# Forget-gate chain of the first head pair moved one token tile earlier, and the decay rows' transfer moved behind three stores

## The chip, the cores and the metric

The program runs on one core of a Trainium2 chip. The metric is the device time of one execution in microseconds; the median of three runs is given. TensorE (PE in the views) multiplies, VectorE (DVE), ScalarE (ACT) and GpSimd (POOL) work elementwise, and SyncE (SP) issues nearly all DMA transfers. Each engine runs its own instructions in program order and waits on semaphores that the other engines raise.

## The reference, cut to what matters

One layer of a hybrid encoder is computed for 1024 prompt tokens and for 8 running streams of 16 tokens with 512 cached tokens each. The part around the change is attention with a forget gate, for 8 heads of width 64:

```python
proj = rms_norm(x, ln1) @ w_in
q, k, v, f, xr, yg = jnp.split(proj, SPLITS, axis=-1)
q = rms_norm(q.reshape(B, T, N_HEADS, HEAD_DIM), q_gain)
k = rms_norm(k.reshape(B, T, N_HEADS, HEAD_DIM), k_gain)
logf = jax.nn.log_sigmoid((f + b_f).astype(jnp.float32))
c = jnp.cumsum(logf, axis=1)
# logit[t,s] = q_t.k_s/sqrt(d) + c_t - c_s, for s <= t
```

After it come a gated recurrence on the other half of the width, an output projection and an MLP of width 4096. The forget values `logf`, their running sums and the normed keys are outputs or operands of the attention.

## The kernel before, in words

The 1152 tokens are nine tiles of 128 (tile 8 holds the streams' tokens). The heads are worked through in four pairs, `p` = 0 to 3. For a pair, TensorE projects tile after tile to queries, keys and values (`project(t)`, 24 matmuls of 384 columns, in four quarters; `amid(t, quarter)` puts other work between the quarters). ScalarE copies the values and squares queries and keys (`sqj`), VectorE sums the squares (`mean(t)`, L1577 and L1578), GpSimd takes the power of -1/2 (L794), VectorE scales queries and keys (`norm(t)`, L1589 and L1591), and TensorE transposes them (`turn_qk(t)`, L2236 and L2237). `turn_qk(t - 1)` stands behind `project(t)`; for `t = 4` it stands behind `project(5)`, and right behind it stands `bound(0, 0)` (L2256), the first product of the turned queries and keys. That product reads the rows of `KA` that hold the running forget sums, and so waits for `c_rows_in`.

Only in pair 0, the forget gate is worked out beside this. `turn(t)` transposes the normed input tiles, ScalarE and VectorE split them in two parts (`turn_hi`, `turn_lo`), `forgets(g)` (16 matmuls, L2094 and L2095) multiplies a third of the tokens with the gate's weights and waits for the low parts of its three tiles, `forget_rows(g)` copies the result, `turn_inputs` (L2101) transposes it. VectorE then computes log-sigmoid in about twenty small operations (`forget_sizes`, `forget_values`, L1460 to L1484), with one exponential on ScalarE in between. `turn_forgets` (L2109, L2113) transposes the values, `prompt_sums` (L1490, L1492) takes the running sums, `prompt_rows` (L1497, L1498) splits them in two parts, `own_sums` (L1504) and `sample_sums` (L1511 to L1521) do the same for the streams. SyncE writes the split rows to a scratch array in device memory (L634, L635), waits for it, and loads two rows per head into `KA` (`decay_rows(0)`, L593).

The order on each engine is the order in which the code is written; there is no planner. SyncE's order in pair 0 is: the nine stores of the forget values (L512), the store of the normed keys of tiles 0 and 1 (`keys_out`, L588, each waits for `norm` of its tile), the two writes and two loads of the decay rows, `keys_out` of tiles 2, 3 and 4, and then the copies of queries and keys that the scores need (`duplicates`, L603 and L604).

Of the kernel before, what the change touches and what calls it, by code (L numbers as in the profile page):

```python
# [7 lines left out]
F32 = mybir.dt.float32  # L8
# [12 lines left out]
H = 8  # L21
# [37 lines left out]
def streaming_step(nc, x_prompt, x_sample, cache_k, cache_v, cache_logf, state_h, state_conv, ln1, w_in, b_f,  # L59
# [36 lines left out]
    c_row = sb(over, "c_row", [40, SEQ], F32R)  # L96
# [134 lines left out]
    c_dram = nc.dram_tensor("c_scratch", [H, 2, SEQ], F32).ap()  # L231
# [272 lines left out]
    with nc.allow_non_contiguous_dma(reason="narrow columns of small arrays"), nc.Block() as block:  # L504

        @block.sync
        def _(sp):
# [83 lines left out]
            def decay_rows(p):  # L591
                for hp in range(2):
                    sp.dma_start(KA[DECAY_ROWS[hp], hp, :].bitcast(F32), c_dram[2 * p + hp]).then_inc(c_rows_in, 16)  # L593
# [32 lines left out]
            def pair_transfers(p):  # L626
                last = p == PAIRS - 1
                keys_out(p, 0)
                if p >= 1:
                    denominators(p - 1)  # L630
                keys_out(p, 1)
                if p == 0:
                    sp.wait_ge(c_split, 1)
                    sp.dma_start(c_dram[:, 0, :], c_row[0:H, :].bitcast(F32)).then_inc(c_saved, 16)  # L634
                    sp.dma_start(c_dram[:, 1, :], c_row[32:32 + H, :].bitcast(F32)).then_inc(c_saved, 16)  # L635
                    sp.wait_ge(c_saved, 32)
                    sp.wait_ge(operands_set, 2)
                    decay_rows(0)
                if p >= 1:
                    sp.wait_ge(s_scores, 2 * p)  # L640
                    past_values(p - 1, 1)
                keys_out(p, 2)
                if p >= 1:
                    quotients(p - 1)
                    for b in range(2):
                        past_keys(p, b)
                keys_out(p, 3)
                keys_out(p, 4)
                if p == 0:
                    sp.wait_ge(stored, 16 * n_stored)  # L650
                    sp.wait_ge(consts_ready, 3)
                duplicates(p, 0)
                for t in range(5, NT):
                    keys_out(p, t)
                    if t == 6 and not last:
                        for j in range(4):
                            sp.wait_ge(w_lo, 4 * p + j + 1)
                            pair_weights(p + 1, j)
                    if t == 6 and last:
                        for u in range(2):  # L660
                            sp.wait_ge(w_lo, 4 * p + u + 1)
                            lru_weights(0, u)
                if p == 0:
                    sp.wait_ge(c_past_ready, 1)
                    for b in range(2):
                        past_keys(0, b)
                duplicates(p, 1)
                sp.wait_ge(v_done, NT * p + NT)
                sp.dma_start(v_prompt[0, 0].rearrange("(t p) h d -> p t h d", p=P)[:, :, 2 * p:2 * p + 2, :].rearrange(
                    "p t h d -> p t (h d)"), v1[:]).then_inc(v_out, 16)  # L670
                sp.dma_start(v_sample[0].rearrange("b t h d -> (b t) h d")[:, 2 * p:2 * p + 2, :],
                             v_own[:].rearrange("p (h d) -> p h d", h=2)).then_inc(v_out, 16)
                for b in range(2, 6):
                    sp.wait_ge(kc_turned, DEC_B * p + b - 1)
                    past_keys(p, b)
                sp.wait_ge(den_done, 6 * p + 6)
                past_values(p, 0)
                if not last:
                    decay_rows(p + 1)
                for b in range(6, DEC_B):  # L680
                    sp.wait_ge(kc_turned, DEC_B * p + b - 1)
                    past_keys(p, b)
                if last:
                    for b in range(4):
                        sp.dma_start(v_last[:, b, :].rearrange("p (t n) -> p t n", t=KP),
                                     cache_v[0, 4 + b, :, 2 * p:2 * p + 2, :].rearrange("(t p) h d -> p t (h d)", p=P)
                                     ).then_inc(vk_in, 16)
# [278 lines left out]
        def _(act):  # L966
# [24 lines left out]
            def first_stage(i):  # L991

                if i == 0:
                    square(0)
                    square(1)
                    turn_hi(0)
                    pair_hi(0, 0)
                    square(2)
                    turn_hi(1)
                    for j in range(1, 4):  # L1000
                        pair_hi(0, j)
                    square(3)
                    turn_hi(2)
                    act.wait_ge(wf_in, 16)
                    nc.scalar.copy(wf[:, :, 0, :], wf_raw[:]).then_inc(wf_split, 1)
                    square(4)
                    turn_hi(3)
                if i == 1:
                    square(5)
                    turn_hi(4)  # L1010
                    square(6)
                    turn_hi(5)
                    square(7)
                    forget_rows(0)
                    turn_hi(6)
                    square(8)
                    forget_rows(1)
                    turn_hi(7)
                    turn_hi(8)
                if i == 2:  # L1020
                    forget_rows(2)
                    act.wait_ge(l_abs, 1)
                    nc.scalar.activation(l_e[:], l_e[:], ACT.Exp, scale=-1.0).then_inc(l_exp, 1)
# [353 lines left out]
        def _(dve):  # L1377
# [35 lines left out]
            def first_stage(i):  # L1413


                if i == 0:
                    for t in range(5):
                        x_mean_of(t)
                        if t >= 2:
                            turn_lo(t - 2)  # L1420
                        if t == 0:
                            dve.wait_ge(ln1_in, 16)
                        x_norm(t)
                        if t == 2:
                            for j in range(4):
                                pair_lo(0, j)
                            dve.wait_ge(wf_split, 1)
                            nc.vector.tensor_tensor(wf[:, :, 1, :], wf_raw[:], wf[:, :, 0, :].bitcast(F32),
                                                    ALU.subtract).then_inc(wf_ready, 1)
                if i == 1:  # L1430
                    x_mean_of(5)
                    dve.wait_ge(small_in, 16 * SMALL)
                    nc.vector.tensor_scalar(qgain[:], qgain[:], DH ** -0.5, None, ALU.mult)
                    dve.wait_ge(rows_turned, 1)
                    nc.vector.tensor_copy(param[:, :, 0:ROWS], psum[:, 5, 0:LC * ROWS].rearrange(
                        "p (c r) -> p c r", c=LC)).then_inc(params_copied, 1)
                    turn_lo(3)
                    x_norm(5)
                if i == 2:
                    for t in (6, 7, 8):  # L1440
                        x_mean_of(t)
                        turn_lo(t - 2)
                        x_norm(t)
                    past_sums()
                    turn_lo(7)
                    turn_lo(8)

            def past_sums():

# [122 lines left out]
            def pair_dve(p):  # L1572
# [85 lines left out]
                for t in range(NT):  # L1658
# [10 lines left out]
                            low_keys(0, hp)  # L1669
                    bounds_ahead(t)  # L1670
                    mean(t)
                    if p == 0 and t == 3:
                        prompt_sums()
                    bounds_behind(t)
                    if p == 0 and t == 0:
                        first_stage(1)
# [1 line left out]
                    if t == 6:  # L1678
                        bound(1, 0)
                    if p == 0 and t == 1:  # L1680
                        forget_sizes()
                        forget_values()
                    if p == 0 and t == 3:
                        prompt_rows()
                        own_sums()
                        sample_sums()
                    if p >= 1 and t == 2:
                        invert(p - 1)
# [351 lines left out]
        def _(pe):  # L2040
# [22 lines left out]
            def first_stage(i):  # L2063
# [4 lines left out]
                if i == 1:  # L2068
# [14 lines left out]
                        last = nc.tensor.transpose(psum[0:64, f_bank(0), kt * P:(kt + 1) * P], cl[:, kt, :], ident[:])  # L2083
                    last.then_inc(c_turned, 1)
                    turn(8)

            def forgets(g):

# [111 lines left out]
            def pair_pe(p):  # L2200
# [130 lines left out]
                        bound(0, 5)  # L2331

                def amid(t, quarter):
                    if p == 0 and (t, quarter) == (2, 0):
                        turn_inputs()
                    if p == 0 and (t, quarter) == (3, 2):
                        turn_forgets()
                    bounds_amid(t, quarter)
                    if (t, quarter) == (8, 2):
                        turn_qk(7)  # L2340

                for t in range(NT):
                    if p == 0:
                        first_stage(t)
                    project(t, amid)
                    if p == 0 and t == 1:
                        forgets(2)
                    if p >= 1:
                        samples_meanwhile(p - 1, t)
                    if 1 <= t < 8:  # L2350
# [330 lines left out]
```

## Time and profile before

| | us |
|---|---|
| median of three runs | 1426.71 (1425.75 to 1428.8) |
| the profiled execution's own time | 1428.8 |
| its span in the trace | 1427.1 |
| TensorE busy | 1369.3 (96%) |
| VectorE busy | 1003.8 (70%) |
| ScalarE busy | 522.7 (37%) |
| GpSimd busy | 389.7 (27%) |

The span is the stretch from the first to the last recorded instruction. A busy share is an average over stages: the first 111 us, in which the changed code lies, have other limits than the MLP that fills the second half. The chain of waits follows the end of the program back through whatever released each step; 85% of the span stands on it for TensorE.

### The profile page before, as it was taken

The page shows a single profiled execution, that of the slowest core. Times are in us where ns is not written, and L with a number is a line of the kernel's source. Part 1 is how long each engine was busy: PE and PEld are TensorE (multiplying, and loading weights), DVE is VectorE, ACT ScalarE, POOL GpSimd, SP SyncE. Part 2 cuts the span into 40 slices and gives each one's busy share as a digit, 9 for nine tenths or more (in the row PEclk, how much of TensorE's full clock was granted, in tenths as well). Part 3 has the DMA queues.
Part 4 walks back from the last instruction along what each step waited for, and adds up shares of the span by engine and source line. Part 5 has one row for each costly group of instructions (what it writes and reads, how often), then busy time and mean ns, then how long its engine had stood idle before and what let it go on. Part 6 is the DMA issues. An engine that isn't in the chain of part 4 may idle for free.

```text
span 1427.1 us, 21431 instructions
## 1 busy us (share of the span) xinstructions
PE 1369.3 (96%) x7479; PEld 1168.0 (82%) x7487; DVE 1003.8 (70%) x1523; ACT 522.7 (37%) x964; POOL 389.7 (27%) x396
## 2 busy tenths in 40 slices
PE   5989999999899999999999999999999999999998
PEld 4765847839658887788999999999999999999997
DVE  6763453543624566765888898888888898888885
ACT  5224242342335555332532343334433343334330
POOL 5310101101100002101532454345433553255320
PEclk9999999999999999999999999999999999999999
DMA  6042333424343032012201110111101110121004
GB/s 200 12 115 74 89 80 111 106 65 113 77 128 84 3 105 87 33 47 89 60 6 53 59 59 27 32 59 59 47 12 59 59 59 0 59 59 59 0 30 133
DMA packets 129544, 92.90 MB, mean 65 GB/s; under 512 B 14678, under 2 KB 119126, under 8 KB 129492
## 3 DMA queue, kind: packets, MB, share of 16 engines
q1 hardware_dynamic: 129492, 92.20, 22.6%
q8 instruction: 33, 0.54, 0.2%
q14 instruction: 19, 0.16, 0.0%
HBM read 78.28 MB, written 9.71 MB: 62 GB/s over the span
## 4 chain that ended last, share of the span: by engine, by line
PE 85%; DVE 5%; DMA 4%; ACT 3%; issue 1%; POOL 1%; SPq 1%; DVEq 0%; POOLq 0%
PE psum L2043 16%; PE psum L2045 15%; PE psum L2044 15%; PE psum L2523 8%; PE psum L2525 8%; PE psum L2524 8%; DMA k_c<-in_cache_k_dram 3%; PE psum L2305 2%; PE psum L2256 2%; PE psum L2287 1%; PE psum L2290 1%; PE psum L2315 1%; PE psum L2414 1%; PE psum L2126 1%; DVE tops L1611 1%
## 5 line engine op out<-in xcount | busy, mean ns | idle before, releaser
L1909 DVE TENSOR_TENSOR mix<-mix,psum 128x512 f32<-128x512 f32 x660 | 417.8, 681 | 92.0 <-PE psum L2525 87.6
L2043 PE MATMUL psum<-h_hi,wu_hi 128*128 128x384 f32 x768 | 259.4, 338 | 0.9 <-DVE wu_lo L1874 0.9
L2045 PE MATMUL psum<-h_hi,wu_lo 128*128 128x384 f32 x768 | 258.1, 336 | 0.0
L2044 PE MATMUL psum<-h_lo,wu_hi 128*128 128x384 f32 x768 | 258.1, 336 | 0.0
L2523 PE MATMUL psum<-wd_hi,u_hi 128*128 128x512 f32 x516 | 201.3, 390 | 0.2 <-DVE mix L1909 0.2
L2525 PE MATMUL psum<-wd_hi,u_lo 128*128 128x512 f32 x516 | 200.7, 389 | 0.0
L2524 PE MATMUL psum<-wd_lo,u_hi 128*128 128x512 f32 x516 | 200.7, 389 | 0.0
L2043 PEld LDWEIGHTS psum<-h_hi,wu_hi 128*128 128x128 f32 x768 | 144.3, 188 | 10.0 <-issue 1.3
L2044 PEld LDWEIGHTS psum<-h_lo,wu_hi 128*128 128x128 f32 x768 | 144.3, 188 | 8.7
L2045 PEld LDWEIGHTS psum<-h_hi,wu_lo 128*128 128x128 f32 x768 | 144.4, 188 | 0.0
L1265 ACT CAST wd_hi<-raw 128x512 fp32r<-128x512 f32 x109 | 67.1, 621 | 179.7 <-PE psum L2525 81.2
L1255 ACT ACTIVATE up<-psum 128x384 f32<-128x384 f32 x96 | 46.8, 487 | 203.0 <-PE psum L2045 167.8
L914 POOL TENSOR_TENSOR up<-up 128x384 f32<-128x384 f32 x15 | 21.1, 1404 | 345.1 <-DVE u_lo L1885 345.1
L2525 PEld LDWEIGHTS psum<-wd_hi,u_lo 128*128 128x128 f32 x516 | 96.9, 188 | 20.6
L2523 PEld LDWEIGHTS psum<-wd_hi,u_hi 128*128 128x128 f32 x516 | 96.9, 188 | 11.9 <-DVE mix L1909 0.6
L2524 PEld LDWEIGHTS psum<-wd_lo,u_hi 128*128 128x128 f32 x516 | 96.9, 188 | 11.2
L2043 PE MATMUL psum<-wp_hi,h_hi 128*128 128x384 f32 x288 | 103.2, 359 | 0.0
L1880 DVE TENSOR_TENSOR wd_lo<-raw,wd_hi 128x512 fp32r<-128x512 f32 x109 | 93.8, 873 | 8.3 <-ACT wd_hi L1265 4.6
L2044 PE MATMUL psum<-wp_lo,h_hi 128*128 128x384 f32 x288 | 98.0, 340 | 0.0
L2045 PE MATMUL psum<-wp_hi,h_lo 128*128 128x384 f32 x288 | 97.9, 340 | 0.0
L794 POOL TENSOR_TENSOR rs<-m,neg_half 128x4 f32<-128x4 f32 x36 | 36.3, 1008 | 190.0 <-DVE m L1578 190.0
L1885 DVE TENSOR_TENSOR u_lo<-up,u_hi 128x768 fp32r<-128x768 f32 (+1 forms) x62 | 75.2, 1213 | 6.2 <-ACT u_hi L1303 5.3
(321 smaller groups left out, 2460.8 us busy)
## 6 DMA issues: line engine op xcount, KB each, us to landing
raw<-in_w_up_dram SPq DMA_DIRECT2D x32, 512.0 KB, 5.9
raw<-in_w_down_dram SPq DMA_DIRECT2D x32, 512.0 KB, 4.4
k_c<-in_cache_k_dram SPq DMA_DIRECT2D x32, 256.0 KB, 2.9
raw<-in_w_in_dram SPq DMA_DIRECT2D x32, 192.0 KB, 4.0
out_dram<-mix SPq DMA_DIRECT2D x9, 512.0 KB
v_c<-in_cache_v_dram SPq DMA_DIRECT2D x16, 256.0 KB, 4.2
raw<-in_w_in_dram SPq DMA_DIRECT2D x8, 512.0 KB, 5.4
raw<-in_w_out_dram SPq DMA_DIRECT2D x8, 512.0 KB, 4.1
```

The source lines that it names most:

```text
L794: nc.gpsimd.tensor_tensor(rs4[:, t % 2, :], m4[:, t % 2, :], neg_half[:], ALU.pow).then_inc(rs4_ready, 1)
L1255: nc.scalar.activation(up[:, into, :], psum[:, bank(m), 0:GN], ACT.Relu).then_inc(up_read, 1)
L1265: nc.scalar.copy(wd_hi[:, slot, :], src).then_inc(wd_rounded, 1)
L1880: nc.vector.tensor_tensor(wd_lo[:, slot, :], src, wd_hi[:, slot, :].bitcast(F32), ALU.subtract).then_inc(wd_ready, 1)
L1885: nc.vector.tensor_tensor(lo, src, hi.bitcast(F32), ALU.subtract).then_inc(u_ready, 1)
L1909: nc.vector.tensor_tensor(half_of(t, half), half_of(t, half), psum[:, product_bank(n), :].rearrange("p (k n) -> p k n", n=P), op).then_inc ...
L2043: nc.tensor.matmul(out, hi(k), r_hi(k), start=first and k == 0, stop=False)
L2044: nc.tensor.matmul(out, hi(k), r_lo(k), start=False, stop=False)
L2045: last = nc.tensor.matmul(out, lo(k), r_hi(k), start=False, stop=end and k == n - 1)
L2523: nc.tensor.matmul(psum[:, bank, :], u_hi, wd_hi[:, w, :], start=first, stop=False)
L2524: nc.tensor.matmul(psum[:, bank, :], u_hi, wd_lo[:, w, :], start=False, stop=False)
L2525: return nc.tensor.matmul(psum[:, bank, :], u_lo, wd_hi[:, w, :], start=False, stop=end)
```

## The change

Nothing is computed in another way; the same instructions are issued in another order on TensorE, ScalarE, VectorE and SyncE, all within pair 0.

```diff
# SyncE, pair_transfers
                 keys_out(p, 1)
-                if p == 0:
-                    sp.wait_ge(c_split, 1)
-                    sp.dma_start(c_dram[:, 0, :], c_row[0:H, :].bitcast(F32)).then_inc(c_saved, 16)
-                    sp.dma_start(c_dram[:, 1, :], c_row[32:32 + H, :].bitcast(F32)).then_inc(c_saved, 16)
-                    sp.wait_ge(c_saved, 32)
-                    sp.wait_ge(operands_set, 2)
-                    decay_rows(0)
...
                 keys_out(p, 3)
                 keys_out(p, 4)
                 if p == 0:
+                    sp.wait_ge(c_split, 1)
+                    sp.dma_start(c_dram[:, 0, :], c_row[0:H, :].bitcast(F32)).then_inc(c_saved, 16)
+                    sp.dma_start(c_dram[:, 1, :], c_row[32:32 + H, :].bitcast(F32)).then_inc(c_saved, 16)
+                    sp.wait_ge(c_saved, 32)
+                    sp.wait_ge(operands_set, 2)
+                    decay_rows(0)
                     sp.wait_ge(stored, 16 * n_stored)
                     sp.wait_ge(consts_ready, 3)
                 duplicates(p, 0)
# ScalarE, first_stage
                     turn_hi(8)
-                if i == 2:
                     forget_rows(2)
                     act.wait_ge(l_abs, 1)
                     nc.scalar.activation(l_e[:], l_e[:], ACT.Exp, scale=-1.0).then_inc(l_exp, 1)
# VectorE, first_stage(2), called ahead of mean(1)
                     turn_lo(8)
+                    forget_sizes()
+                    forget_values()
# VectorE, loop over tiles
                     mean(t)
-                    if p == 0 and t == 3:
-                        prompt_sums()
...
                     norm(t)
...
                     if p == 0 and t == 1:
-                        forget_sizes()
-                        forget_values()
-                    if p == 0 and t == 3:
+                        prompt_sums()
                         prompt_rows()
                         own_sums()
+                    if p == 0 and t == 3:
                         sample_sums()
# TensorE, first_stage(1), called ahead of project(1)
                     turn(8)
+                    forgets(2)
# TensorE, amid
-                    if p == 0 and (t, quarter) == (2, 0):
+                    if p == 0 and (t, quarter) == (1, 0):
                         turn_inputs()
-                    if p == 0 and (t, quarter) == (3, 2):
+                    if p == 0 and (t, quarter) == (2, 2):
                         turn_forgets()
# TensorE, loop over tiles
                     project(t, amid)
-                    if p == 0 and t == 1:
-                        forgets(2)
```

On SyncE, in the transfers of pair 0, the rows before are these (`c_row` holds the split running sums, `qk` the normed queries and keys of a tile):

```order
L512 DMA out_dram<-l_f 128x8 x9
L588 DMA out_dram<-qk 128x128 x2
L634 DMA c_scratch<-c_row 8x1024
L635 DMA c_scratch<-c_row 8x1024
L593 DMA KA<-c_scratch 2x1024 x2
L588 DMA out_dram<-qk 128x128 x3
L603 DMA cross_qk<-QA 64x512
```

And these are the rows of the changed kernel:

```order
L512 DMA out_dram<-l_f 128x8 x9
L588 DMA out_dram<-qk 128x128 x5
L644 DMA c_scratch<-c_row 8x1024
L645 DMA c_scratch<-c_row 8x1024
L593 DMA KA<-c_scratch 2x1024 x2
L603 DMA cross_qk<-QA 64x512
```

The decay rows' four transfers stand behind the key stores of tiles 2, 3 and 4, no longer ahead of them.

On VectorE, behind the small operations of the forget values, the rows before are these (each pair L1577, L1578 is a `mean`, each pair L1589, L1591 a `norm`; the first ones here are those of tile 2):

```order
L1484 TENSOR_SCALAR param<-param 128x4x2
L1577 TENSOR_REDUCE s<-sqj 128x4
L1578 TENSOR_SCALAR m<-s 128x4
L1589 TENSOR_TENSOR qk<-psum,rs 128x256
L1591 TENSOR_TENSOR qk<-qk,kgain 128x128
L1577 TENSOR_REDUCE s<-sqj 128x4
L1578 TENSOR_SCALAR m<-s 128x4
L1490 SCALAR_TENSOR_TENSOR cp<-ones_w,psum 8x512
L1492 SCALAR_TENSOR_TENSOR cp<-ones_w,cp,psum 8x512
L1589 TENSOR_TENSOR qk<-psum,rs 128x256
L1591 TENSOR_TENSOR qk<-qk,kgain 128x128
L1497 TENSOR_SCALAR c_row<-cp 8x1024
```

And in the changed kernel, where the first `mean` and `norm` are those of tile 1:

```order
L1484 TENSOR_SCALAR param<-param 128x4x2
L1577 TENSOR_REDUCE s<-sqj 128x4
L1578 TENSOR_SCALAR m<-s 128x4
L1589 TENSOR_TENSOR qk<-psum,rs 128x256
L1591 TENSOR_TENSOR qk<-qk,kgain 128x128
L1490 SCALAR_TENSOR_TENSOR cp<-ones_w,psum 8x512
L1492 SCALAR_TENSOR_TENSOR cp<-ones_w,cp,psum 8x512
L1497 TENSOR_SCALAR c_row<-cp 8x1024
L1498 SCALAR_TENSOR_TENSOR c_row<-cp,c_row 8x1024
L1504 TENSOR_REDUCE c_new<-psum 64x16
L1577 TENSOR_REDUCE s<-sqj 128x4
L1578 TENSOR_SCALAR m<-s 128x4
```

The small operations now stand ahead of tile 1's `mean`, which was ahead of them, and the running sums stand in one block behind tile 1's `norm`, ahead of tile 2's `mean`.

## Rows read from the trace of the kernel before

**Rows 1.** Busy times by stretch: length, PE, PEld, DVE, ACT, POOL, PEclk, DMA.
```profile
69.60:73.70 4.10, 0.00 (x0) 0.00 (x0) 2.77 (x7) 0.65 (x2) 1.01 (x1) 1.00 0.13 36
73.70:78.10 4.40, 4.36 (x18) 4.33 (x19) 4.09 (x8) 0.00 (x0) 0.61 (x1) 0.61 0.58 134
```

**Rows 2.** Chain of waits, 40 to 112 us: start, length, engine, tile, line.
```profile
70.73 0.48 DVE c_past L1521
...
71.89 1.02 POOL rs L794
```

**Rows 3.** TensorE's timeline: start, length, engine, line; in brackets idle before, releaser.
```profile
29.17 1.97 PE L2059 MATMUL psum<-ident,x_more 128*128 128x128 f32 x8 [2.82 <-DVE x_more L1389]
...
41.30 1.09 PE L2059 MATMUL psum<-ident,x_in 128*128 128x128 f32 x8 [1.35 <-DVE x_in L1389]
...
46.41 0.33 PE L2094 MATMUL psum<-h_hi,wf 128*16 128x384 f32 x1
...
50.56 0.72 PE L2101 MATMUL psum<-ident,f_rows 16*128 16x16 f32 x9
...
57.81 1.03 PE L2109 MATMUL psum<-ident,l_f 128*8 128x128 f32 x8
...
60.30 0.27 PE L2236 MATMUL psum<-ident,qk 128*128 128x128 f32 x1
...
69.25 0.34 PE L2045 MATMUL psum<-wp_hi,h_lo 128*128 128x384 f32 x1
73.74 0.33 PE L2236 MATMUL psum<-ident,qk 128*128 128x128 f32 x1 [4.16 <-DVE qk L1591]
...
73.93 0.30 PE L2256 MATMUL psum<-KA,QA 128*128 128x128 f32 x1
```

**Rows 4.** VectorE's timeline.
```profile
42.30 2.45 DVE L1396 TENSOR_TENSOR h_lo<-psum,h_hi 128x512 fp32r<-128x512 f32 x4
...
51.33 0.23 DVE L1460 TENSOR_TENSOR l_in<-psum,bf_b 128x72 f32<-128x72 f32 x1 [1.47 <-PE psum L2101]
...
57.20 0.42 DVE L1577 TENSOR_REDUCE s<-sqj 128x4 f32<-128x256 f32 x1
...
61.62 1.20 DVE L1490 TENSOR_TENSOR_SCAN cp<-ones_w,psum 8x512 f32<-8x512 f32 x1
...
64.16 0.43 DVE L1589 TENSOR_TENSOR qk<-psum,rs 128x256 f32<-128x256 f32 x1
...
64.83 0.67 DVE L1497 TENSOR_SCALAR c_row<-cp 8x1024 fp32r<-8x1024 f32 x1
...
67.11 0.24 DVE L1511 TENSOR_TENSOR_SCAN cc_new<-ones_w,cc,c_new 64x16 f32<-64x16 f32 x1
...
71.14 0.41 DVE L1577 TENSOR_REDUCE s<-sqj 128x4 f32<-128x256 f32 x1
...
73.39 0.29 DVE L1591 TENSOR_TENSOR qk<-qk,kgain 128x128 f32<-128x128 f32 x1
```

**Rows 5.** ScalarE's timeline, the squares of tile 3.
```profile
60.66 0.39 ACT L1090 ACTIVATE sqj<-psum 128x256 f32<-128x256 f32 x1
```

**Rows 6.** GpSimd's timeline, the end of the second stream mask.
```profile
52.06 0.38 POOL L855 CAST smask<-build 128x128 bf16<-128x128 f32 x1
```

**Rows 7.** SyncE's timeline: start and length of the issues.
```profile
66.78 0.30 SPq L634 DMA_DIRECT2D c_scratch<-c_row  x1
67.12 0.29 SPq L635 DMA_DIRECT2D c_scratch<-c_row  x1
69.22 0.52 SPq L593 DMA_DIRECT2D KA<-c_scratch  x2
...
73.71 0.33 SPq L588 DMA_DIRECT2D out_dram<-qk  x1
```

**Rows 8.** The key stores' view: issue to landing, 55 to 112 us.
```profile
out_dram<-qk SPq DMA_DIRECT2D x9, 64.0 KB, 1.6
```

**Rows 9.** Chain of waits, the longest load of cached keys.
```profile
134.58 4.67 DMA k_c<-in_cache_k_dram
```

## The prediction

> **What bounds the kernel now.** I read the page first: TensorE is busy for 96% of the span, so only its idle stretches and its slow stretches can change the time, and an edit on another engine counts only if it makes or removes such a stretch. Then I read TensorE's timeline from the start to 111 us, where all the changed code runs. Between the end of the input tiles' transposes and the first attention product it has one large hole: `project(5)` ends at 69.25 + 0.34 = 69.59, and `turn_qk(4)` starts at 73.74, after 4.16 us of idle [rows 3]. The table by stretch shows the same, and that the clock granted in the next stretch, 4.40 us long, is 0.61 of full, a mixture of the 1.2 and the 2.4 GHz level [rows 1]. That stretch loses 4.40 x (1 - 0.61) = 1.7 us. Hole and slow stretch together are 5.9 us; this is all that the change could win there.
>
> The chain of waits says what ends the hole: VectorE's `sample_sums` end at 70.73 + 0.48 = 71.2, then `mean(4)`, GpSimd's power (1.02 us), `norm(4)` [rows 2], which ends at 73.39 + 0.29 = 73.68 [rows 4]. So VectorE's queue is the limit there, not a transfer. `bound(0, 0)` follows at 73.93 [rows 3] without a wait of its own: the decay rows were issued to `KA` by 69.22 + 0.52 = 69.74 [rows 7]. They are not on the path before. I call the end of `norm(4)` N, and compare the start of `bound(0, 0)`, 73.93 before, since everything behind it keeps its order.
>
> **The change part by part.** First, `forgets(2)` ahead of `project(1)`. It waits for the low parts of tile 8. TensorE's transposes end at 41.30 + 1.09 = 42.39 [rows 3], VectorE's four splits at 42.30 + 2.45 = 44.75 [rows 4]. Before, `project(1)` lay in this gap. Now nothing does: TensorE is idle for 2.4 us, with 24 ready projection matmuls queued behind the waiting instruction. This is a new cost.
>
> Second, where this puts the forget chain. From the first matmul of `forgets(2)` to `turn_inputs` the trace has 50.56 - 46.41 = 4.15 us; a `turn_qk` of 0.13 us in it is gone (an estimate, half of the 0.27 us of such a row). So `turn_inputs` starts at 44.8 + 4.0 = 48.8, and VectorE, which starts 51.33 - 50.56 = 0.77 behind it, at 49.6: 1.7 us earlier than the 51.33 of before [rows 3, 4].
>
> Third, VectorE from there to N. The blocks, with their lengths from [rows 4]:
> - forget values: 57.20 - 51.33 = 5.87, to 55.5
> - tile 1, `mean` to the end of `norm`: 73.68 - 71.14 = 2.54 (of which 1.2 us is waiting for GpSimd), to 58.0
> - `prompt_sums`: 64.16 - 61.62 = 2.54, to 60.55
> - `prompt_rows` and `own_sums`: 67.11 - 64.83 = 2.28, to 62.85
> - tile 2: 2.54, to 65.4
> - tile 3: 2.54, to 67.95
> - `sample_sums`: 71.14 - 67.11 = 4.03, to 72.0
> - tile 4: 2.54, so N = 74.55
>
> That is 0.9 us later than 73.68, though the forget chain began 1.7 us earlier. Two things eat the lead: tile 1's `mean` and `norm` now stand behind the forget values instead of ahead of them (2.54 us more), and the two scans no longer lie between `mean(3)` and `norm(3)`, where they covered GpSimd's 1.2 us. Against it, VectorE's wait of 1.3 us for tile 3's squares is gone. None of the blocks has to wait longer for its input: the squares of tile 3 stood ready 60.66 + 0.39 = 61.05, 0.75 us after the `turn_qk(2)` behind that projection began [rows 3, 5], and each projection now ends at least 1 us ahead of its `mean`; `turn_forgets`, at 57.81 before [rows 3], comes 1.7 us earlier and ends, with its last product, near 57.5, ahead of the 58.0 at which the scans want it. GpSimd's second mask ends at 52.44 before [rows 6], and now stands behind tile 1's power, to end near 60.8, ahead of tile 2's `mean` at 62.85.
>
> Fourth, TensorE on the way to N. From 42.39 to `turn_qk(2)` at 60.30 it works without a hole [rows 3], 17.9 us; the same work is there after the change. So it reaches `turn_qk(2)` at 42.39 + 2.4 + 17.9 = 62.7 and there waits for tile 2's `norm` at 65.4: a second new hole of 2.7 us. From there 69.59 - 60.30 = 9.3 us bring it to 74.7, the same moment as N. The hole of 4.16 us ahead of `turn_qk(4)` is really gone, and has been paid for by 5.1 us of holes earlier.
>
> Fifth, the decay rows, the dearest edit. Their four transfers now stand on SyncE behind `keys_out(4)`, which waits for N. `bound(0, 0)` needs them. From N [rows 7]: the key store is issued from 0.03 to 0.36; the two writes to the scratch array take 67.41 - 66.78 = 0.63 and end at 1.03; SyncE then waits for them to land, 69.22 - 67.41 = 1.81, to 2.84; the second load is issued from 3.1. Its landing is not in the trace. The nearest rows bound it: a key store lands 1.6 us after its issue [rows 8], the second scratch write was landed 69.22 - 67.12 = 2.1 us after it began [rows 7], and as an upper end stands the 4.67 us of the longest load of cached keys [rows 9]. The decay load is two rows of one head, far smaller than that, so I take 1.6 to 2.1 and say 1.85. The rows are there at N + 5.0 = 79.55, with 4.67 at 82.3. TensorE has only `turn_qk(4)` to do meanwhile, 0.2 us, so it is idle for about 4.7 us where it was idle for 4.16. I cost the key stores that now go ahead at nothing: nobody but `norm(5)` to `norm(8)` waits for them, over 5 us later.
>
> The Trainium skill, in "DMA: Bandwidth & Descriptors", section "Anatomy of one DMA — SWDGE (gpsimd) path", gives a fixed cost of about 2.0 us for each DMA, nearly all of it the wait for the write's receipt, whatever the size. The 2.1 us of the scratch write [rows 7] agrees; by the page the rows would be there at about N + 5.1, which changes nothing.
>
> **The sum.** `bound(0, 0)` at 79.55 against 73.93: +5.6 us. The same by holes: 2.4 + 2.7 + 4.7 - 4.16 = 5.6. Behind it the slow stretch of 1.7 us stays as it is, since the hole in front of it is no shorter. VectorE is ahead of TensorE there, but what follows the hole is limited by TensorE's projections. So the profiled execution would take 1428.8 + 5.6 = 1434.4. That execution lies 2.1 us above the median of its three runs; for the median I forecast 1426.7 + 5.6 = 1432.3.
>
> **The rivals.**
> - The slow clock comes early. After 2.82 us of idle the eight transposes at 29.17 took 1.97 us, after 1.35 us of idle those at 41.30 took 1.09 [rows 3]. The new hole of 2.4 us follows one of 1.35 with 1.09 of work between, and lies between these two cases. If `forgets(2)` runs at 1.2 GHz, the forget chain and N move by as much: half to all of the 1.7 us of [rows 1], say 1.5. Then 1433.8. The hole at `turn_qk(2)` can slow `project(4)` and `project(5)` too, but TensorE arrives there when the decay rows still need 5 us, so that costs nothing.
>
> The Trainium skill, "TensorE: Matmul & The Clock Gate", section "HAM oscillation — how this bites in real kernels", says that waits between groups of matmuls put the array back to half clock each time, which speaks against two more holes; the 29.17 row agrees, the 41.30 row shows a short wait that did not.
>
> - The clock does not fall at the last hole, and the slow stretch of before goes. For it: the trace shows falls behind 2.82 and 4.16 us of idle and none behind 1.35 [rows 3], too few to call it certain. Against it: 4.7 us is more than either. It gives back 1.7: 1430.6.
> - The shift is swallowed later. Behind pair 0's attention the chain stands on loads of cached keys, up to 4.67 us each [rows 9]. If their end were set by an earlier time than TensorE's, the 5.6 us would vanish in them: 1426.7. Against it: each of these loads waits for the transposes of the load two before it (`kc_turned`), so they move with TensorE. Only the first two are issued freely.
> - The other side: VectorE runs ahead as the order intends, `turn_qk(2)` does not wait, and the decay rows are in place. Then the old 5.9 us go and only the 2.4 us come: 1423.2. It decides at N + 5.0 < 73.9, so N would have to be under 68.9, 5.7 us earlier than worked out; that would need two whole tiles' `mean` and `norm` and more to vanish from VectorE's queue. Nothing in the rows speaks for it except that the forget chain does start earlier.
>
> **How the numbers follow.** The forecast gets 0.55, the early slow clock 0.24, the unchanged fast clock 0.11, the swallowed shift 0.05, the other side 0.04, and 0.01 is for none of them. A change of less than 0.2%, 2.9 us, can't be told from none here. Slower than that are the first two, and most of the third: 0.88. Within it lie the swallowed shift and a bit of the third: 0.08. Faster: 0.04. The range runs from 1429.6 (the third case less 1.0 for the spread of a median) to 1436.0 (the second with a landing nearly 1 us later and the spread). With the upper end of the landing alone the time would be 1435.1, inside it.
>
> **What would show it.** In the changed kernel's profile: an idle of about 2.4 us ahead of the `forgets(2)` matmuls, and of about 2.7 ahead of the third `turn_qk`; `turn_qk(4)` near 74.7 with almost no wait; SyncE's writes to the scratch array at about 75, no longer at 66.8, though `c_row` is ready near 62.5; and a wait of nearly 5 us ahead of the first L2256 row, ended by the DMA into `KA`. It would be wrong if the first L2256 product started before 77, if the decay rows were issued ahead of N, or if the time behind this product grew or shrank by more than 2 us.

## The result and the profile after

The changed kernel takes 1440.31 us (median of four runs, 1440.14 to 1440.63) against 1427.76 for the kernel before on the same chip (four runs, 1425.75 to 1429.01). The ratio is 1.0085 with an interval of 1.0068 to 1.0102: slower, as forecast, but by 12.5 us where 5.6 were forecast, and outside the range given. Two more comparisons of the same two kernels (below) gave 1.0051 and 1.0057, 7.8 and 7.9 us between the medians. The profiled execution takes 1439.09 us (span 1437.4), 10.3 more than the 1428.8 of before; this difference the trace can explain.

The head of the page of the changed kernel shows busy time, share of the span and instructions of each engine:

```profile
span 1437.4 us, 21430 instructions
...
PE 1376.5 (96%) x7479; PEld 1172.7 (82%) x7487; DVE 1003.8 (70%) x1523; ACT 522.7 (36%) x964; POOL 389.7 (27%) x396
```

VectorE and GpSimd are busy for exactly as long as before. TensorE is busy 7.2 us longer than its 1369.3, though its work is the same. So most of what was lost is not waiting: TensorE ran slower.

The table by stretch says where. These are two stretches of the kernel before, cut at the end of `turn(8)` and at the first `bound(0, 0)` product (columns as in [rows 1]):

```profile
42.40:73.90 31.50, 27.23 (x164) 24.32 (x164) 21.04 (x56) 6.57 (x18) 8.97 (x20) 1.00 0.07 13
73.90:113.50 39.60, 35.91 (x196) 25.16 (x195) 26.07 (x46) 11.85 (x29) 4.03 (x4) 0.96 0.39 104
```

And the same two of the changed kernel:

```profile
42.70:82.10 39.40, 31.49 (x166) 27.26 (x165) 24.23 (x61) 6.43 (x18) 9.71 (x21) 0.86 0.07 12
82.10:123.00 40.90, 37.16 (x194) 26.11 (x194) 22.96 (x40) 11.80 (x29) 3.21 (x4) 0.92 0.38 99
```

In the first, the time grows by 7.9 us; 4.3 of these are busy time (27.23 to 31.49) at a granted clock of 0.86 where it was 1.00. In the second it grows by 1.3. The remaining 1.1 us are spread over the rest of the span, 0.3 of them ahead of `turn(8)`.

TensorE's timeline of the changed kernel shows the holes (start, length, tile, count, in brackets the idle time before and what ended it), in answer to [rows 3]:

```profile
41.62 1.09 PE L2056 MATMUL psum<-ident,x_in 128*128 128x128 f32 x8 [1.36 <-DVE x_in L1387]
...
45.21 0.48 PE L2092 MATMUL psum<-h_hi,wf 128*16 128x384 f32 x1 [2.50 <-DVE h_lo L1394]
...
51.72 0.73 PE L2099 MATMUL psum<-ident,f_rows 16*128 16x16 f32 x9
...
68.26 0.47 PE L2234 MATMUL psum<-ident,qk 128*128 128x128 f32 x1 [2.23 <-DVE qk L1591]
...
78.54 0.27 PE L2234 MATMUL psum<-ident,qk 128*128 128x128 f32 x1
82.15 0.48 PE L2254 MATMUL psum<-KA,QA 128*128 128x128 f32 x1 [3.23 <-DMA KA<-c_scratch]
```

The reader is to see three holes, of 2.50, 2.23 and 3.23 us, at the three places named in the prediction, and also that the first matmul behind each of them takes 0.47 or 0.48 us, where the same kinds took 0.33, 0.33 and 0.30 in [rows 3]. The stretches behind them say how long that lasted:

```profile
45.20:50.60 5.40, 5.39 (x17) 2.74 (x18) 0.00 (x0) 0.07 (x1) 0.55 (x2) 0.50 0.00 0
...
68.20:74.40 6.20, 6.14 (x29) 6.11 (x30) 4.71 (x12) 0.06 (x1) 1.01 (x1) 0.74 0.08 21
82.10:88.50 6.40, 6.35 (x22) 5.64 (x23) 2.09 (x6) 0.00 (x0) 0.20 (x1) 0.50 0.40 92
```

0.50 is 1.2 GHz throughout. The losses, length times what is missing from 1.00, are 5.4 x 0.50 = 2.7, 6.2 x 0.26 = 1.6 and 6.4 x 0.50 = 3.2 us; before there was one such stretch, of 1.7. The sum: holes 2.50 + 2.23 + 3.23 - 4.16 = 3.8, slow clock 2.7 + 1.6 + 3.2 - 1.7 = 5.8, together 9.6, against 7.9 + 1.3 = 9.2 by stretch.

VectorE's timeline carries the first of these losses on to N:

```profile
52.48 0.23 DVE L1460 TENSOR_TENSOR l_in<-psum,bf_b 128x72 f32<-128x72 f32 x1 [7.42 <-PE psum L2099]
...
64.07 1.22 DVE L1498 SCALAR_TENSOR_TENSOR c_row<-cp,c_row 8x1024 fp32r<-8x1024 f32 x1
...
74.92 0.42 DVE L1577 TENSOR_REDUCE s<-sqj 128x4 f32<-128x256 f32 x1 [0.23 <-ACT sqj L1088]
...
77.19 0.29 DVE L1591 TENSOR_TENSOR qk<-qk,kgain 128x128 f32<-128x128 f32 x1
```

The forget chain begins at 52.48, not 49.6, and N is 77.19 + 0.29 = 77.48. `c_row` is ready at 64.07 + 1.22 = 65.29. SyncE's timeline shows when it is written out:

```profile
63.01 14.84 SPq L588 DMA_DIRECT2D out_dram<-qk  x5
77.89 0.34 SPq L644 DMA_DIRECT2D c_scratch<-c_row  x1
78.27 0.29 SPq L645 DMA_DIRECT2D c_scratch<-c_row  x1
80.35 0.52 SPq L593 DMA_DIRECT2D KA<-c_scratch  x2
```

The rows lie ready for 12.6 us behind key stores that wait for N, and then the two dependent transfers follow, which the chain of waits times from issue to landing:

```profile
78.27 2.07 DMA c_scratch<-c_row
80.35 0.22 SPq L593
80.62 1.48 DMA KA<-c_scratch
82.15 0.48 PE psum L2254
```

The product starts 82.15 - 77.48 = 4.67 us behind N.

### The profile page after: what moved, and what is told of

It reads as the page before. It is cut to its first block, busy times and chain, and to the rows that moved or that the text cites. A ratio compares the mean times of both kernels' runs of the same rounds, so it can differ in the third digit from the quotient of the medians.

```text
span 1437.4 us, 21430 instructions
## 1 busy us (share of the span) xinstructions
PE 1376.5 (96%) x7479; PEld 1172.7 (82%) x7487; DVE 1003.8 (70%) x1523; ACT 522.7 (36%) x964; POOL 389.7 (27%) x396
## 4 chain that ended last, share of the span: by engine, by line
PE 86%; DVE 5%; DMA 4%; ACT 2%; POOL 1%; issue 1%; SPq 1%; DVEq 0%; POOLq 0%
PE psum L2040 16%; PE psum L2041 16%; PE psum L2042 16%; PE psum L2519 8%; PE psum L2521 8%; PE psum L2520 8%; DMA k_c<-in_cache_k_dram 3%; PE psum L2303 2%; PE psum L2254 2%; PE psum L2285 1%; PE psum L2288 1%; PE psum L2313 1%; PE psum L2410 1%; PE psum L2124 1%; DVE tops L1611 1%
```

## The experiments

Each kernel from e1 on was timed in five rounds beside the kernel before, on the same chip within a group. "Stretch" is from the start of the last input tiles' transposes to the first product of the second half of pair 0's attention, from one profile each; 67.2 us before. It leaves out what the rest of the kernel does from run to run, and so separates the causes better than the medians. It is one execution each, though, and inside it too the clock falls in some executions and not in others, for 1 us or more; where that happened is said below.

| kernel | median, us | before, us | ratio, 95% | stretch |
|---|---|---|---|---|
| changed, first | 1440.31 | 1427.76 | 1.0085 (1.0068 to 1.0102) | +9.2 |
| changed, second | 1438.60 | 1430.84 | 1.0051 (1.0035 to 1.0067) | +8.7 |
| changed, third | 1438.67 | 1430.72 | 1.0057 (1.0041 to 1.0072) | +9.4 |
| e1 decay rows back | 1433.38 | 1430.31 | 1.0025 (1.0015 to 1.0034) | +1.8 |
| e2 decay rows alone | 1434.53 | 1430.31 | 1.0032 (1.0021 to 1.0042) | +4.6 |
| e3 one hole filled | 1436.09 | 1430.31 | 1.0040 (1.0025 to 1.0055) | +6.2 |
| e4 three holes filled | 1433.97 | 1430.31 | 1.0026 (1.0015 to 1.0037) | +3.5 |
| e8 e1 and e3 together | 1430.00 | 1430.84 | 0.9996 (0.9984 to 1.0008) | +0.8 |
| e9 `forgets(2)` alone | 1437.97 | 1430.72 | 1.0052 (1.0034 to 1.0071) | +7.0 |
| e10 e9, hole filled | 1434.69 | 1430.72 | 1.0028 (1.0016 to 1.0040) | +4.4 |
| e6 sums in pieces | 1427.62 | 1430.84 | 0.9977 (0.9966 to 0.9989) | -3.1 |
| e7 all interleaved | 1427.51 | 1430.84 | 0.9974 (0.9963 to 0.9985) | -3.6 |

Five expectations missed in size. The second run of the changed kernel came out 7.8 us above the kernel before and not 10 to 12, e9 7.3 above and not 5, e10 4.0 above and not 2.5, e6 3.2 us faster and not 4, and e7 3.3 us faster and not 5. The others came out near what their first theory said.

**The decay rows.** e1 is the changed kernel with SyncE's block put back:

```diff
                 keys_out(p, 1)
+                if p == 0:
+                    sp.wait_ge(c_split, 1)
+                    ... two writes to c_dram, the wait for them, operands_set
+                    decay_rows(0)
```

> The changed kernel with the decay rows' four transfers back ahead of the key stores of tiles 2, 3 and 4; all else as changed. My theory: the 3.2 us hole ahead of the first L2254 product goes, and with it the half-clock stretch of 6.4 us behind it (3.2 us lost); the hole ahead of the third turn_qk (2.2 us) and the half-clock forgets stay. So about 6.4 us less than the changed kernel, 1434. Rival (the late rows cost only their wait, the clock falls anyway after the holes before): 3.2 us less, 1437. Rival (VectorE's order alone sets the end): no gain, 1440.

e2 is the kernel before with only this block moved behind `keys_out(4)`.

> The kernel before with only the decay rows' four transfers moved behind the key store of tile 4. Theory: norm(4) ends at 73.7 as before and the first attention product starts 4.7 us behind it, at 78.3, not 73.9: +4.4 us, and the half-clock stretch behind it may grow from 1.7 to 3.2 us lost: +4.4 to +5.9, about 1433. Rival (the late rows only hurt together with the other order): under +2.

Of the stretch's 9.2 us e1 leaves 1.8, a difference of 7.4. Not all of it is the edit: the third `turn_qk` starts 68.10 - 42.64 = 25.46 us behind the start of the stretch in e1 and 68.26 - 41.62 = 26.64 in the changed kernel, so 1.2 us were gained ahead of anything that the edit touches, since the slow clock at `forgets(2)` ended sooner (below). That leaves 6.2. The same edit between e3 and e8 takes 6.2 - 0.8 = 5.4. TensorE's timeline of e1:

```profile
68.10 0.33 PE L2235 MATMUL psum<-ident,qk 128*128 128x128 f32 x1 [2.24 <-DVE qk L1592]
...
77.25 0.30 PE L2255 MATMUL psum<-KA,QA 128*128 128x128 f32 x1
```

The first product follows without a wait, and the table by stretch grants it the full clock:

```profile
76.00:84.00 8.00, 6.89 (x42) 6.02 (x41) 6.59 (x14) 0.55 (x2) 1.22 (x2) 1.00 0.35 82
```

Alone, the edit costs 4.6 us. TensorE's timeline of e2 has the old hole and a second one right behind it:

```profile
75.19 0.48 PE L2235 MATMUL psum<-ident,qk 128*128 128x128 f32 x1 [4.17 <-DVE qk L1590]
...
79.94 0.47 PE L2255 MATMUL psum<-KA,QA 128*128 128x128 f32 x1 [4.06 <-DMA KA<-c_scratch]
```

The 4.6 us are the new hole of 4.06 and `turn_qk(4)` between the two holes at the low clock, 79.94 - 75.19 - 4.06 = 0.7 us where it had 0.2 [rows 3]. The slow stretch behind them is worth what it was before, 7.00 x 0.24 = 1.7:

```profile
80.00:87.00 7.00, 7.00 (x34) 6.56 (x34) 2.50 (x6) 0.00 (x0) 0.00 (x0) 0.76 0.33 77
```

The edit is worth more inside the changed kernel, 5.4 to 6.2, since there it also brings a hole and a slow stretch where e1 has neither.

**The clock behind the first hole.** e3 is the changed kernel with 14 matmuls, whose results are overwritten, in the hole ahead of `forgets(2)`; they start right behind the transposes of `turn(8)`, last 2.69 us in the trace, and end when the low parts of tile 8 are there (`forgets(2)` starts 3.59 us behind the start of the stretch, with them and without):

```diff
                     turn(8)
+                    pe.wait_ge(params_copied, 1)
+                    filler(5, 1, 14)     # 14 matmuls of 128x384 into a bank not yet in use
                     forgets(2)
```

> The changed kernel with 14 extra matmuls (results thrown away) in the 2.5 us hole ahead of forgets(2). Theory: the array stays at 2.4 GHz, the 16 forget matmuls take 2.8 us and not 5.4, and everything up to norm(4) moves 2.6 us earlier: about 1437.5. Rival (the hole, not the clock, is what costs): no change, 1440.

e4 also fills the other two holes, with 12 matmuls ahead of `turn_qk(2)` and 18 ahead of `bound(0, 0)`.

> As the run with 14 extra matmuls, and 12 more in the hole ahead of the third turn_qk and 18 more in the hole ahead of the first attention product, all results thrown away. Theory: also the half-clock stretch behind the last hole (3.2 us lost) goes, and the waits themselves stay: about 1434.5, 5.8 under the changed kernel. Rival (holes alone): 1440, or more where a filler outlasts its hole.

Neither lets any useful work start earlier; they only keep TensorE busy. With the first hole filled the stretch shrinks by 3.0 us (9.2 to 6.2; 2.5 against the second trace of the changed kernel, in which as in e3 the clock stayed up behind the second hole), with all three by 5.7. In e4 the clock is never low between `turn(8)` and the end of the stretch; one row of the table by stretch:

```profile
66.00:78.00 12.00, 11.29 (x66) 10.68 (x64) 9.18 (x20) 3.29 (x8) 1.93 (x3) 1.00 0.09 18
```

So the slow clock costs the changed kernel 5.7 us, and without it 3.5 of the 9.2 are left. These 3.5 are not all that comes from later starts: in e4 `bound(0, 0)` starts 78.39 - 40.71 = 37.68 us behind the start of the stretch, against 32.63 before, which is 5.0 later, and 1.6 are won back behind it, where the kernel before has its own slow stretch and e4 has none.

**`forgets(2)` alone.** e9 is the kernel before with only `forgets(2)` moved ahead of `project(1)`, e10 the same with the filler of e3.

> The kernel before with one edit: forgets(2) stands ahead of project(1), as in the changed kernel; all other orders as before. Theory: the 2.5 us hole and the half-clock stretch behind it (2.7 us) push project(1), its norm and the forget chain back alike: +5 us. Rival (only the hole counts, the clock recovers within the hole of 4.2 us that was there): +2.5. Rival (TensorE has slack up to norm(4), so part of it is swallowed in that hole): under +2.

> The same with 14 extra matmuls in the hole, results thrown away. Theory: the clock stays, the hole's 2.5 us stay: +2.5 us against the kernel before, 2.7 under the run without the extra matmuls. Rival (clock without effect): the same as that run.

TensorE's timeline of e9 behind the hole:

```profile
45.23 0.48 PE L2095 MATMUL psum<-h_hi,wf 128*16 128x384 f32 x1 [2.50 <-DVE h_lo L1396]
...
46.14 0.52 PE L2096 MATMUL psum<-h_lo,wf 128*16 128x384 f32 x1
46.46 0.52 PE L2095 MATMUL psum<-h_hi,wf 128*16 128x384 f32 x1
```

And of e10:

```profile
46.15 0.34 PE L2101 MATMUL psum<-h_hi,wf 128*16 128x384 f32 x1
46.32 0.33 PE L2102 MATMUL psum<-h_lo,wf 128*16 128x384 f32 x1
```

The same matmuls follow each other every 0.32 us in e9 and every 0.17 us in e10. The filler takes 2.6 us off the stretch (7.0 to 4.4). The part that was wrong in the sum is measured here by itself, with all other orders as before. The whole 7.0 us of e9 are more than its two terms: `turn_qk(4)` starts 5.4 us later from the start of the stretch (79.47 - 41.63 against 73.74 - 41.30), which is the hole of 2.50, the 2.6 of the clock and 0.3, and another 1.6 are lost behind it. e10 has the same 1.6 (4.4 less the 77.07 - 41.85 - 32.44 = 2.8 of its `turn_qk(4)`), behind a hole of 3.83 us in both. In e9 1.0 of the 1.6 is lost by the eighth `turn_qk` (it starts 98.93 - 41.63 = 57.30 us behind the start of the stretch, and 50.91 before, 6.4 later), in e10 0.7, with a longer slow stretch behind the hole; the rest is lost behind a wait of 1.32 us near the end, where the clock falls again in these two and did not in the kernel before (see e6 below). e9's table by stretch, with the slow stretch of either place:

```profile
46.00:52.00 6.00, 6.00 (x23) 3.73 (x21) 0.00 (x0) 0.00 (x0) 0.00 (x0) 0.59 0.00 0
78.00:84.00 6.00, 4.54 (x17) 4.44 (x18) 4.81 (x10) 0.00 (x0) 1.41 (x2) 0.52 0.42 98
```

**What the new orders are worth.** e8 has the decay rows back and the first hole filled.

> The changed kernel with the decay rows' transfers back and with 14 extra matmuls in the hole ahead of forgets(2). Theory: of the 9 to 12 us only the hole at the third turn_qk and its slow stretch remain, against the gone hole of before: 1 us faster than before to 1 slower. Rival (VectorE's new order costs by itself, whatever the clock): 3 us or more slower than before, as the run with the rows back alone.

Its ratio, 0.9996 (0.9984 to 1.0008), can't be told from no change, and its stretch is 0.8 us longer: two holes, ahead of `forgets(2)` (filled, but still time lost) and of 2.25 us ahead of `turn_qk(2)` (here the clock fell behind it, 0.72 in the 6.1 us that follow), have taken the place of the one of 4.16. So the shorter wait ahead of `turn_qk(4)` is paid for earlier, even with the transfers and the first clock fall out of it.

The table also parts the two halves of what e8 keeps. e9 has `forgets(2)` early and nothing else, +7.0; e1 adds the new orders of VectorE and ScalarE and the earlier `turn_inputs` and `turn_forgets`, and stands at +1.8. With the hole filled the same step leads from +4.4 (e10) to +0.8 (e8). So these orders win 3.6 to 5.2 us (some 1.2 of the 5.2 being the shorter slow stretch of e1), and it is the place of `forgets(2)` that costs more than they win.

**The changed kernel again.** It was run twice more, since the first comparison gave more than its trace.

> The changed kernel itself, unedited, beside the other kernels of this call on the same chip: 10 to 12 us above the kernel before, the same three holes (2.5, 2.2 and 3.2 us) and three half-clock stretches as in its first trace. If the first comparison was inflated by chance it comes out nearer to 9.

> The changed kernel, unedited, a third time, to size it: the first comparison gave a ratio of 1.0085, the second 1.0051. Theory from the traces (the stretch from the last input tile's transposes to the second half of the attention is 8.7 to 9.2 us longer): +8 to +10 us. If it comes out at +12 again, something outside that stretch has a part.

The three traced stretches agree (+9.2, +8.7, +9.4); the medians say +12.5, +7.8 and +7.9. One thing differs inside. TensorE's timeline of the second:

```profile
67.43 0.33 PE L2234 MATMUL psum<-ident,qk 128*128 128x128 f32 x1 [2.23 <-DVE qk L1591]
...
71.89 0.27 PE L2234 MATMUL psum<-ident,qk 128*128 128x128 f32 x1
...
81.12 0.47 PE L2254 MATMUL psum<-KA,QA 128*128 128x128 f32 x1 [4.29 <-DMA KA<-c_scratch]
```

And of the third:

```profile
68.70 0.47 PE L2234 MATMUL psum<-ident,qk 128*128 128x128 f32 x1 [2.24 <-DVE qk L1591]
...
74.64 0.27 PE L2234 MATMUL psum<-ident,qk 128*128 128x128 f32 x1
...
82.68 0.47 PE L2254 MATMUL psum<-KA,QA 128*128 128x128 f32 x1 [3.27 <-DMA KA<-c_scratch]
```

After the same idle time of 2.2 us the clock fell in one and not in the other: one projection takes 71.89 - 67.43 = 4.5 us or 74.64 - 68.70 = 5.9. It costs little (the stretches differ by 0.6 and 0.8 us), since TensorE is early there, and the last hole is 1.0 us shorter where the projection is slower.

**A faster order.** The hole of [rows 2, 3] is there because `sample_sums`, eight small operations, stand in one block ahead of `mean(4)`. e6 is the kernel before with that block cut into four:

```diff
                     bounds_ahead(t)
+                    if p == 0 and t >= 6:
+                        sample_sums(t - 5)
                     mean(t)
...
                         own_sums()
-                        sample_sums()
+                        sample_sums(0)       # the scan, its copy, the high parts
```

> The kernel before with sample_sums cut in four: the first three operations stay where they were, the other five stand ahead of the mean of tiles 6, 7 and 8. Theory (VectorE's queue sets the end of norm(4), and the decay rows' round trip comes next): norm(4) ends 3.1 us earlier at 70.6, the rows land near 71.6, the 4.2 us hole shrinks to some 2 us in two parts and the half-clock stretch (1.7 us) goes: 4 us faster than before. Rival (the pieces are paid back behind, where TensorE waits for VectorE's maxima): no change.

e7 adds the idea of the change without its hole: `forgets(2)` in the middle of `project(1)`, the forget values half ahead of `norm(1)`, and the blocks behind them spread over tiles 2 and 3.

> What the change tried, in another order: the last forgets between the quarters of project(1), turn_inputs in its third quarter gap, the forget values interleaved with tile 1's mean and norm, running sums behind tile 2's norm, decay rows' transfers where they were before, sample_sums in four pieces. Theory: no hole over 1 us from tile 1 to the first attention product, which starts near 70.3 and not 73.9, at full clock: 5 us faster than before. Rival (the forget values ahead of tile 1's norm make new waits for TensorE): within 1 us of before or slower.

Both beat the kernel before, at ratios of 0.9977 and 0.9974, 3.2 and 3.3 us between the medians; the two can't be told apart. In e7 TensorE reaches the first product with no hole:

```profile
70.41 0.27 PE L2248 MATMUL psum<-ident,qk 128*128 128x128 f32 x1
...
70.54 0.30 PE L2268 MATMUL psum<-KA,QA 128*128 128x128 f32 x1
```

The 5.9 us that the prediction named as all there was to win have shrunk to 3.6 in the stretch. Part of the rest is new waiting. e6 stops for 1.18 us ahead of `turn_qk(4)` and for 0.98 us at the maxima of the scores, where the kernel before ran on without a wait at half clock:

```profile
70.36 0.33 PE L2242 MATMUL psum<-ident,qk 128*128 128x128 f32 x1 [1.18 <-DVE qk L1595]
...
74.44 0.42 PE L2262 MATMUL psum<-KA,QA 128*128 128x384 f32 x1 [0.98 <-DVE tops L1615]
```

The other part is the clock again, in a place where TensorE's own order is the same in all runs. TensorE's timeline of the kernel before, at the first product of the second half of the attention:

```profile
105.26 0.73 PE L2256 MATMUL psum<-KA,QA 128*128 128x512 f32 x2 [1.32 <-DVE tops L1611]
...
108.52 0.47 PE L2287 MATMUL psum<-QA,KA 128*128 128x512 f32 x1 [0.76 <-DVE QA L1615]
108.83 0.40 PE L2290 MATMUL psum<-cross_qk 128*128 128x512 f32 x1
```

And of e6:

```profile
101.73 0.73 PE L2262 MATMUL psum<-KA,QA 128*128 128x512 f32 x2 [1.32 <-DVE tops L1615]
...
105.06 0.77 PE L2293 MATMUL psum<-QA,KA 128*128 128x512 f32 x1 [0.65 <-DVE QA L1619]
105.63 0.63 PE L2296 MATMUL psum<-cross_qk 128*128 128x512 f32 x1
```

The waits are the same or shorter, yet the granted clock is 1.00 from 105 to 112 us before and 0.52 from 104 to 111 in e6, a loss of 7.00 x 0.48 = 3.4 us; in e7 it is 0.54 from 101 to 108.5. It fell here in four of the thirteen traces (e6, e7, e9 and e10); why in these is not shown. Most of this loss lies behind the end of the stretch: at the ninth `turn_qk`, which starts 115.62 - 41.30 = 74.32 us behind the start of the stretch before, e6 is only 1.2 us ahead (113.97 - 40.90 = 73.07) and e7 2.9 (112.71 - 41.27 = 71.44), and the whole spans are 1.3 and 0.6 us shorter. That both are faster rests on the medians (12, 11 and 28 runs) and not on the traces.

## Why the prediction was right in direction and wrong in size

| step | forecast | measured |
|---|---|---|
| hole ahead of `forgets(2)` | 2.4 | 2.50 |
| start of the forget chain on VectorE | 49.6 | 52.48 |
| N | 74.55 | 77.48 |
| hole ahead of `turn_qk(2)` | 2.7 | 2.23 |
| start of `turn_qk(4)` | 74.7 | 78.54 |
| `bound(0, 0)` behind N | 5.0 | 4.67 |
| last hole | 4.7 | 3.23 (4.29 in the second) |
| start of `bound(0, 0)` | 79.55 | 82.15 |
| slow stretch behind it, loss against before | 0 | 1.5 |

- **The places of the holes, and what ends them, were right.** All three are where they were put. So was the dearest edit: the decay rows are issued behind N, 12.6 us after they are ready, and the landing took 1.48 us where 1.6 to 2.1 were taken. e1 and e2 show that this edit is the cause of the last hole.
- **The step that failed is the clock at `forgets(2)`.** The likeliest case left it at 2.4 GHz and gave the fall a chance of 0.24 and a price of 1.5 us. It fell in all five traces that have this hole unfilled (the changed kernel three times, e1 and e9, each with 2.50 us of idle), and in the first trace it cost 2.7: 16 matmuls at 0.32 instead of 0.17 us each make 2.4, and the start of the next projection the rest. By the start of the first `turn_qk`, the changed kernel's three traces are 2.3 to 2.7 us behind e3 and e9 is 2.6 behind e10; in e1 only the first ten matmuls were slow, and there it is 1.4. e3 and e10, in which the hole was filled and all else left, give 3.0 and 2.6 back. The rival's mechanism was right, and its price of 1.5, from half to all of the 1.7 us of [rows 1], was read off a stretch that was only partly slow (e1 alone comes near it); a hole is to be priced by how much work runs behind it at half speed. N was late by 0.3 (the start) + 2.4 to 2.6 (the clock) + 0.2 (VectorE's wait for tile 4's squares, at 74.92), which is the 2.9 between 74.55 and 77.48.
- **"Behind it the slow stretch of 1.7 us stays as it is" failed too.** It lasted 6.4 us at 0.50, a loss of 3.2. The reason given, that the hole in front is no shorter, does not bound the stretch behind it: that hole was shorter (3.23) and the stretch longer. With these two terms the forecast would have been 5.6 + 2.6 + 1.5 = 9.7 us, against 9.2 in the stretch.
- **That a slow `project(4)` costs nothing was nearly right.** The second run of the changed kernel has it fast and the others slow, and the stretches differ by 0.6 and 0.8 us. Of this 0.3 to 0.4 were there already at the first `turn_qk`; the rest, 0.3 to 0.4, goes with VectorE's wait of 0.23 and 0.28 us for tile 4's squares, which the second run does not have.
- **The rival without a fall behind the last hole** is what e4 makes by force. It stands at +3.5 us in the stretch and +3.7 in the median; the prediction gave it 1430.6 - 1426.7 = 3.9. The sum by idle time alone was therefore near: 5.6 for the start of `bound(0, 0)`, where e4 has 5.0. It was the clock that was mis-sized.
- **The swallowed shift and the other side did not happen.** What `bound(0, 0)` loses is still there at the end of the span (9.2 of 10.3 us in the stretch). VectorE got no lead: N is later, not earlier, although the new orders by themselves bring it forward (35.17 us behind the start of the stretch in e10, 33.42 in e8; 32.38 before).

**What stays open.** The first comparison says 12.5 us, the two others 7.8 and 7.9 where the kernel before took 1430.8 us instead of 1427.8, and the trace of the first 10.3. The two terms that failed bring the forecast rise from 5.6 to 9.7 us; the 2.8 us from there to 12.5 are not accounted for. The kernel before itself ranges from 1425.75 to 1434.9 us, and its time follows the mean granted clock: 1426.28 at 0.996, 1434.88 at 0.989, and over the 70 runs beside e1 to e11 the correlation is -0.89. The four runs of the changed kernel in the first comparison stood at 0.985 to 0.987, those of the second at 0.987 to 0.991 and of the third at 0.985 to 0.992, and one further run of the first comparison, not in its median, took 1437.16 us at 0.989, so a lower clock goes with the larger number; the clocks of the kernel before in that comparison are not on record, but for the 0.994 of its profile. How long a slow stretch lasts differs between executions of the same code; that this made the first comparison larger was not shown.

## What to carry to other kernels

Price a transfer that is moved in a queue by the wait it now stands behind, and then by its whole chain to the consumer: here two dependent small transfers cost 4.6 us behind a wait that was on the critical path. Price a new hole of over 2 us on TensorE at its length and, where work on the critical path follows it, up to about as much again for slow work (here 1.4 to 2.7 us behind 2.50, 3.2 behind 3.23, but 1.7 behind 4.16), unless something else keeps the engine busy. Where one engine's block of small operations makes a hole, cut the block into pieces and put them into its idle slots; bringing the whole chain forward won 3.6 to 5.2 us on VectorE's side and lost 7.0 with the product that had to come first.

## What the runs showed of the hardware

- A hole of 2.50 us on TensorE, 1.09 us of work behind one of 1.36, brought the clock to 1.2 GHz in five of five traces (in the first a granted 0.50 for 5.4 us, in e1 0.51 for 3.2), while the hole of 1.35 us alone, before, did not. A wait of 1.32 us near the end of the stretch stands in all thirteen traces, and in four of them the clock fell at it or within 3 us (a granted 0.52 for 7 us in e6). The rule cited in the prediction from the Trainium skill, "TensorE: Matmul & The Clock Gate", section "HAM oscillation — how this bites in real kernels", that waits between groups of matmuls bring back the half clock each time, held for this hole, although the waits in the page's example are longer. It did not hold each time for the one of 2.2 us ahead of the third `turn_qk`: the clock fell behind it in two of three traces of the changed kernel, and in three of the six traces that have it unfilled (not in e1 and e3, but in e8).
- 14 matmuls without use, 2.69 us in the trace, put into the hole of 2.50, kept the clock at 2.4 GHz in four of four traces (e3, e4, e8, e10), and gave back 2.6 to 3.0 us, where the prediction priced the fall at 1.5.
- The slow stretch behind holes of 3 to 4 us was worth 1.7 us in the kernel before (4.16 us idle) and 3.2 in the changed one (3.23 us idle). Behind 3.83 us of idle in e9 it was 6.60 x 0.43 = 2.8. Its length does not follow from the hole.
- A small write to DRAM took 2.07 us from issue to landing, the load of it back 1.48. The 2.0 us with which the prediction checked the load's landing fits the write and is too long for the load.
